# Modulation vectors: four column-tiled rows and a transpose in place of sixteen one-column matmuls

## What is computed

```python
def modulation(cond, w_ada, b_ada):
    m = jax.nn.silu(cond) @ w_ada + b_ada
    return [t[..., None, :] for t in jnp.split(m, 6, axis=-1)]

def modulate(h, shift, scale):
    return h * (1 + scale) + shift
```

## Time and profile before

| | us |
|---|---|
| median of 3 runs | 2021.09 |
| lowest, highest | 2018.03, 2022.53 |
| the profiled execution, its device time | 2019.94 |
| its span, first to last instruction | 2018.1 |
| PE busy | 1816.4 (90%) |
| DVE busy | 1369.9 (68%) |
| ACT busy | 799.4 (40%) |
| POOL busy | 153.7 (8%) |

### The profile page before, as it was taken

How to read it: one execution, slowest core, us unless ns; L and a number is a source line. 1 busy time by engine, 2 the same in 40 slices (tenths; PEclk the granted TensorE clock), 3 DMA queues, 4 the chain that set the end, 5 groups by cost and what they waited for, 6 DMA issues and landing times. The chain is left out here.

```text
span 2018.1 us, 28781 instructions
## 1 busy us (share of the span) xinstructions
PE 1816.4 (90%) x11914; PEld 1623.7 (80%) x11914; DVE 1369.9 (68%) x1856; ACT 799.4 (40%) x1138; POOL 153.7 (8%) x156
## 2 busy tenths in 40 slices
PE   5788989899999999779899998955899999898999
PEld 1578668678788878676789998954899999788999
DVE  2596565889966775664567666889787876755544
ACT  1321454343213431334455455352443434445452
POOL 0123100011000110141001010001000001100000
PEclk9778679899999999787999999986899999889999
DMA  6342100334364445330034644623687885313552
GB/s 246 142 167 87 60 1 22 146 145 162 141 233 186 181 162 194 128 142 25 10 131 149 205 145 161 251 102 122 236 328 296 327 323 186 109 53 136 189 185 86
DMA packets 46658, 317.87 MB, mean 158 GB/s; under 512 B 5248, under 2 KB 6272, under 8 KB 12608
## 3 DMA queue, kind: packets, MB, share of 16 engines
q1 hardware_dynamic: 45936, 312.22, 42.2%
q0 software_dynamic: 592, 3.81, 0.5%
HBM read 314.96 MB, written 1.05 MB: 157 GB/s over the span
## 5 line engine op out<-in xcount | busy, mean ns | idle before, releaser
L1375 PE MATMUL PM<-Hhi,whi 128*128 128x256 f32 (+1 forms) x1766 | 567.3, 321 | 72.3 <-DVE Hlo L1247 31.0
L1376 PE MATMUL PM<-Hlo,whi 128*128 128x256 f32 (+1 forms) x1766 | 554.8, 314 | 0.0
L1377 PE MATMUL PM<-Hhi,wlo 128*128 128x256 f32 (+1 forms) x1766 | 554.8, 314 | 0.0
L873 DVE TENSOR_TENSOR wlo<-raw,whi 128x2048 fp32r<-128x2048 f32 (+3 forms) x205 | 443.0, 2161 | 139.2 <-ACT whi L621 138.9
L621 ACT ACTIVATE whi<-raw 128x2048 fp32r<-128x2048 f32 (+3 forms) x205 | 365.2, 1781 | 187.0 <-PE PM L1377 159.1
L1375 PEld LDWEIGHTS PM<-Hhi,whi 128*128 128x128 f32 x1766 | 344.8, 195 | 102.0 <-issue 53.6
L1376 PEld LDWEIGHTS PM<-Hlo,whi 128*128 128x128 f32 x1766 | 346.4, 196 | 17.0 <-issue 0.2
L1377 PEld LDWEIGHTS PM<-Hhi,wlo 128*128 128x128 f32 x1766 | 345.6, 196 | 17.6
L902 DVE SCALAR_TENSOR_TENSOR acc<-raw,silc,acc 128x512 f32<-128x512 f32 x384 | 286.1, 807 | 1.6 <-DVE wlo L873 0.2
L1375 PE MATMUL PM<-Ghi,whi 128*128 128x256 f32 (+1 forms) x864 | 270.8, 313 | 11.7 <-DVE Glo L1099 11.7
L1376 PE MATMUL PM<-Glo,whi 128*128 128x256 f32 (+1 forms) x864 | 265.7, 308 | 0.0
(11 more groups left out here) (186 smaller groups left out, 1998.2 us busy)
## 6 DMA issues: line engine op xcount, KB each, us to landing
raw<-in_ada SPq DMA_DIRECT2D x104, 1024.0 KB, 4.8
raw<-in_wm SPq DMA_DIRECT2D x91, 1024.0 KB, 4.9
raw<-in_wl SPq DMA_DIRECT2D x68, 1024.0 KB, 4.9
raw<-in_wl SPq DMA_DIRECT2D x32, 704.0 KB, 4.4
raw<-in_wm SPq DMA_DIRECT2D x8, 704.0 KB, 4.1
raw<-in_wm SPq DMA_DIRECT2D x4, 768.0 KB, 4.9
X<-in_x SPq DMA_DIRECT2D x1, 2048.0 KB, 9.4
bias<-in_bias POOLq DMA_DIRECT2D x1, 2048.0 KB, 11.2
```

Source lines behind the costliest of these rows:

```text
L873: dve.tensor_tensor(wslot(wlo, i, usize(u)), slot_raw(n, usize(u)), wslot(whi, i, usize(u)).bitcast(F32), ALU.subtract)\
L1375: pe.matmul(out, st_hi, mv_hi, start=first, stop=False)
L1376: pe.matmul(out, st_hi, mv_lo, start=False, stop=False)
L1377: return pe.matmul(out, st_lo, mv_hi, start=False, stop=last)
```

## The change

The two halves of a vector are now summed together. The four slots of `acc` are summed over the partitions as four rows: for each slot one matmul with a 128 x 32 block of ones as weights and the slot's 512 columns as moving operand, written to its own 32 partitions of one PSUM bank (`ada_rows`, one call for a vector). ACT copies the bank to a new buffer `rsum`. One unit later PE transposes the four 128 x 128 blocks of `rsum` (`ada_columns`), so that the sums stand on the partitions, and DVE adds the bias; for vectors with two partial sums it now adds the two on the columns. Pieces 16 to 19 move: two behind unit 8 and two behind unit 9, where there were one, one, and two behind unit 10. The first piece of a vector now waits for the rows of the one before, since all four slots are read at once; before, it waited for the `ada_sum` two halves back. The diff below is in the order of the file: the plan, then ACT (behind `evac(u)`), DVE (`ada`, then `ada_done`) and PE.

```diff
+    n[8] = n[9] = 2
+    n[10] = 0
...
-REDUCE_AT = [[a // 2 for a in (ADA_AT[i - 1] if i else []) if a % 2] for i in range(NU)]
+ROWS_AT = [[a // 4 for a in (ADA_AT[i - 1] if i else []) if a % 4 == 3] for i in range(NU)]
+COLUMNS_AT = [ROWS_AT[i - 1] if i else [] for i in range(NU)]
...
+                    for v in ROWS_AT[i]:
+                        act.wait_ge(*at("aux", ("rows", v)))
+                        if v > 2:
+                            act.wait_ge(*at("aux", ("ada", v - 1)))
+                        act.activation(rsum[:, :], aux(("rows", v)), ACT.Copy).then_inc(*tick("aux_act", ("rows", v)))
...
-                if part == 0 and hv >= 2:
-                    dve.wait_ge(*at("aux", ("ada", hv - 2)))
+                if part == 0:
+                    dve.wait_ge(*(at("aux", ("rows", v - 1)) if v > 2 else at("aux", ("ada", ("first", 3)))))
...
+                each = view(aux(key), "p (k h w z) -> p h w k z", k=4, h=2, w=2)[:, :, :, :, 0]
+                srcv, odd = each[:, :, 0:nw], each[:, :, 1:2]
+                for h in range(2):
+                    ins = dve.tensor_tensor(dst[:, h], srcv[:, h], bia[:, h].unsqueeze(1).to_broadcast([P, nw, 4]), ALU.add)
+                if nw == 1:
+                    ins.then_inc(*C.link("dve_chain"))
+                    dve.wait_ge(*C.last)
+                    for h in range(2):
+                        ins = dve.tensor_tensor(dst[:, h], dst[:, h], odd[:, h], ALU.add)
...
-            def ada_sum(hv):
+            def ada_rows(v):
+                key = ("rows", v)
+                dst = take(key)
+                for hv in (2 * v, 2 * v + 1):
+                    pe.wait_ge(*at("raw_used", RAW_AT["ada", 2 * hv + 1]))
+                for r in range(4):
+                    ins = pe.matmul(dst[32 * r:32 * r + 32, :], ones[:, 0:32], acc[:, r * 512:r * 512 + 512], start=True, stop=True)
+                ins.then_inc(*tick("aux", key))
+
+            def ada_columns(v):
+                key = ("ada", v)
+                dst = take(key)
+                pe.wait_ge(*at("aux_act", ("rows", v)))
                 for c in range(4):
-                    for who in range(2):
-                        a = (hv % 2) * 1024 + who * 512 + c * 128
-                        if v < CTXV:
-                            ins = pe.matmul(dst[:, who * 4 + c:who * 4 + c + 1], acc[:, a:a + 128], ones[:, 0:1], start=True, stop=True)
-                        else:
-                            ins = pe.matmul(dst[:, c:c + 1], acc[:, a:a + 128], ones[:, 0:1], start=(who == 0), stop=(who == 1))
+                    ins = pe.transpose(dst[:, c * 128:c * 128 + 128], rsum[:, c * 128:c * 128 + 128], ident)
                 ins.then_inc(*tick("aux", key))
...
-                    for hv in REDUCE_AT[i]:
-                        ada_sum(hv)
+                    for v in ROWS_AT[i]:
+                        ada_rows(v)
+                    for v in COLUMNS_AT[i]:
+                        ada_columns(v)
```

More of the change, by code:

```diff
@@ L224, in ada_plan @@
     for st in ("L0", "L1", "M1"):
-        assert sum(n[:first_of("out", st)]) % 2 == 0
+        at_attn = first_of("out", st)
+        assert (len(ADA_FIRST) + sum(n[:at_attn])) % 4 == 0 and n[at_attn - 1] == n[at_attn - 2] == 0
     return out
@@ L907, in ada, with mod_of, ada_first_done @@
                         marks[half] = C.last
-            def ada_done(hv):
+            def mod_of(v):
+                base = {0: 0, 1: 6, 2: 12, 3: 18, 4: 20}[0 if v < 6 else 1 if v < 12 else 2 if v < 18 else 3 if v < 20 else 4]
+                return MODTYPE[v - base]
+            def ada_first_done(hv):
                 v, half = hv // 2, hv % 2
-                key = ("ada", hv)
+                key = ("ada", ("first", hv))
+                dve.wait_ge(*at("aux", key))
+                dst = view(mod[:, v * 16:v * 16 + 16], "p (w k) -> p w k", w=2)[:, :, half * 4:half * 4 + 4]
+                srcv = view(aux(key, 0, 8), "p (k w) -> p w k", w=2)
+                bia = feat[:, FEAT["bada"] + v * 8 + half * 4:FEAT["bada"] + v * 8 + half * 4 + 4].unsqueeze(1).to_broadcast([P, 2, 4])
+                dve.tensor_tensor(dst, srcv, bia, ALU.add).then_inc(*tick("aux_dve", key))
+                if mod_of(v) == "scale":
+                    dve.wait_ge(*at("aux_dve", key))
+                    g = feat[:, FEAT["norm"] + half * 4:FEAT["norm"] + half * 4 + 4].unsqueeze(1).to_broadcast([P, 2, 4])
+                    dve.scalar_tensor_tensor(out=dst, in0=dst, scalar=1.0, in1=g, op0=ALU.add, op1=ALU.mult)\
+                        .then_inc(*tick("mod", v if half else ("half", v)))
@@ L913, in ada_done @@
+            def ada_done(v):
+                key = ("ada", v)
                 dve.wait_ge(*at("aux", key))
                 nw = 2 if v < CTXV else 1
[L915 to L922, removed]
+                dst = view(mod[:, v * 16:v * 16 + 8 * nw], "p (w h k) -> p h w k", w=nw, h=2)
+                each = view(aux(key), "p (k h w z) -> p h w k z", k=4, h=2, w=2)[:, :, :, :, 0]
@@ L923, in ada_done @@
+                ins.then_inc(*tick("aux_dve", key))
+                if mod_of(v) == "scale":
                     norm = {1: 0, 4: 1, 7: 2, 10: 3, 13: 4, 16: 5, 19: 6, 21: 7, 24: 8}[v]
-                    ins.then_inc(*tick("aux_dve", key))
                     dve.wait_ge(*at("aux_dve", key))
-                    g = feat[:, FEAT["norm"] + norm * 8 + half * 4:FEAT["norm"] + norm * 8 + half * 4 + 4].unsqueeze(1).to_broadcast([P, nw, 4])
-                    ins = dve.scalar_tensor_tensor(out=dst, in0=dst, scalar=1.0, in1=g, op0=ALU.add, op1=ALU.mult)
@@ L928, in ada_done @@
-                    ins.then_inc(*tick("mod", v if half else ("half", v)))
-                else:
-                    ins.then_inc(*tick("aux_dve", key))
+                    g = feat[:, FEAT["norm"] + norm * 8:FEAT["norm"] + norm * 8 + 8].unsqueeze(1).to_broadcast([P, nw, 8])
+                    both = view(mod[:, v * 16:v * 16 + 8 * nw], "p (w k) -> p w k", w=nw)
+                    dve.scalar_tensor_tensor(out=both, in0=both, scalar=1.0, in1=g, op0=ALU.add, op1=ALU.mult).then_inc(*tick("mod", v))
```

13 lines of the change are left out of this document (6 added, 7 removed).

## The result

| | before | after |
|---|---|---|
| median of 4 runs, us | 2021.81 | 1966.17 |
| lowest, highest | 2018.03, 2023.91 | 1965.05, 1967.2 |
| profiled execution, its device time | 2019.94 | 1967.2 |
| its span | 2018.1 | 1965.4 |
| mean granted clock over the span | 0.915 | 0.924 |

The ratio of after to before is 0.9727, with a 95% interval of 0.971 to 0.9744: about 55 us faster. The direction was right; the forecast of 1980 and the low end of its range, 1971, were both too high. Between the profiled executions the gain is 52.7 us, where the sum gave 39.8.

The account below looks back on a forecast made before the run. PE, busy 90% of the span, was taken as the bound in most stretches. Saving 34.3 us there plus 7 in L0's projections, less 0.5 and 1, gave 39.8: from 2019.94 to 1980 us, own range 1971 to 1990, with rivals to 2009.

Parts of the forecast that it names:

- the 34 old calls that were priced: One-column reduction calls in PE-bound stretches, taken at 1.78 us each; with one more at 0.8, 60.5 us.
- the five in L0's `up`: Old reduction calls in a DVE-bound stretch, 420 to 536 us, where a shorter PE gains nothing: worth 0.
- Rival 1: Column tiles overlap only in part: 19 to 29 us more than forecast, 1999 to 2009 us; chance 0.15.
- rival 2: fp32 column tiles don't overlap at all, rows cost 3.65 us, slower than before: 2037 us; chance 0.13.
- Rival 3: In M0's MLP and KV, DVE or the DMAs become the bound, 16 us lost: 1996 us; chance 0.08.
- Step (a): L0's projections, call at 131.57: rows of vector 2 take 2.0 us instead of 3.22; 1.3 us gained.
- Step (b): L0's projections, behind unit 4: no reduction there any more, so unit 5 starts at 166.2, 4.8 us earlier.
- R: PE time of one vector's rows, four column tiles together: 1.07 us at full clock, bounds 0.9 and 3.65.
- The break-even: Price of a vector's rows at which the time equals the old kernel's: near 2.9 us.
- unit 156: The call behind it, ahead of a norm, covers DVE and ACT work awaited anyway: 0.8 us, not 1.78.
- (c): L0's projections, call at 200.50: rows of vector 3 take 2.0 us instead of 3.41; 1.4 us gained.
- the 1 us set aside: Allowance for added ACT copies, DVE sums and waits, and DMA share, otherwise counted as covered: 1 us.

Follow-up runs that it names:

- e3: Changed kernel with the four row matmuls writing the same 128 partitions one after the other, 128 columns of ones as weights: 2022.06 us, ratio 1.0002 to the kernel before.
- e1: The changed kernel again, unchanged, for a second profile: 1965.94 us, ratio 0.973 to the kernel before.
- e5: Kernel before with the one reduction behind unit 4 moved behind unit 5: 2012.85 us, ratio 0.9969.
- e6: Kernel before with only pieces 16 to 19 placed as in the change: 2020.6 us, ratio 1.0009.
- e2: Changed kernel with the eight row matmul records issued twice: 1986.16 us, ratio 0.983 to the kernel before.
- e9: Kernel before with one more DVE memset over 1024 columns ahead of the first projection unit, about 0.9 us: 2018.22 us, ratio 0.9979.
- e10: Kernel before with one more DVE memset over 2048 columns ahead of the first projection unit, about 1.8 us: 2020.6 us, ratio 0.9991.
- e8: The kernel before again, unchanged, for a second profile: 2018.87 us, ratio 0.9997.
- e11: Changed kernel with one more DVE memset over 1024 columns ahead of the first projection unit: 1966.92 us, ratio 0.9727 to the kernel before.
- e12: Changed kernel with one more DVE memset over 2048 columns ahead of the first projection unit: 1966.4 us, ratio 0.9723 to the kernel before.
- e14: Changed kernel with the four transposes of one vector moved from behind unit 41 to behind unit 42: 1973.58 us, ratio 0.9771 to the kernel before.
- e7: Kernel before with each reduction cut from 8 one-column matmuls to 1, vectors wrong: 1951.84 us, ratio 0.9677.
- e13: Kernel before with one call of ada_sum moved from behind unit 42 to behind unit 43: 2016.9 us, ratio 0.9982.
- e4: Changed kernel with only the first of the four row matmuls, 128 columns of ones, other slots left out: 1962.85 us, ratio 0.9712 to the kernel before.

## Why the prediction was off

**Right.** The bound and the counts: the 34 old calls that were priced are on the path, none of the five in L0's `up` is. The tiles: the records start in two groups of four, 0.46 us apart, the next unit's load 1.00 us behind the first (forecast 1.07). The transposes 0.43. Rival 1 and rival 2 fell; e3 is rival 2 made real, and it ends at the time of before, not above it. Rival 3 did not occur in M0's MLP. Step (a): PE got to unit 3 1.3 us earlier, as forecast (0.7 in e1). Step (b), 4.8 us at unit 5: measured 4.8, and e5 shows it alone. The moved pieces: at most 0.3 in e6, 0.5 forecast.

**The price of rows, mis-sized against the change.** I took R from load to load. On the path the rows cost 1.19 and not 1.07, because turning costs 0.34 and not 0.2; 18 times 0.12 is 2.2 us of gain less. Eight old calls in M0 cost 1.87 and not 1.78, 0.7 us the other way.

**The break-even, mis-sized.** I gave 2.9 us for R. e3, at 3.43, ends level. By the slope of 24 measured in e2, (3.43 - 1.19) x 24 is 54 us, all of the gain. The break-even was low because the rest of the gain was larger than I had it. (The low end of the forecast's own range does not follow from its terms either: 1980.1 - 3 - 5 is 1972, not 1971.)

**Rival 3's mechanism, at a place I had not named.** In the recurrent stage I counted 4.1 us gained and 1.5 came. Up to `lgate` and in `lout` 4.7 us was gained, and 1.5 went back to the wait for `wlo` and 1.6 ahead of the norm. The earlier trace rows count calls by stretch and do not show what waits behind them: I should have followed each stretch to the next wait, as I did for unit 156.

**A call put at nothing.** The forecast gave 0 to the call "in L1 behind a wait for POOL". PE behind unit 55, in before and in after:

```profile
896.29 0.93 PE L1452 MATMUL PX<-cst,zu 128*128 128x128 f32 x4 [3.20 <-POOL zu L564]
897.02 3.47 PE L1467 MATMUL PX<-cst,acc 128*128 128x1 f32 x16
900.34 0.56 PE L1375 MATMUL PM<-whi,Hhi 128*128 128x256 f32 x1
```

```profile
868.23 1.11 PE L1484 MATMUL PX<-cst,zu 128*128 128x128 f32 x4 [3.21 <-POOL zu L570]
869.27 1.94 PE L1495 MATMUL PX<-acc,cst 128*32 128x512 f32 x8
871.14 0.47 PE L1407 MATMUL PM<-whi,Hhi 128*128 128x256 f32 x1
```

The wait stands ahead of the transposes; the call comes behind it, at half clock, and unit 56 starts when it ends. It took 3.32 us, the rows take 1.87: 1.4 us gained on the path.

**The step that failed: the clock was held fixed.** The sum gave ordinary work the time that it took at the clock it had before; (a) and (c) priced their rows at half clock. Most of the surplus sits where that clock changed:
- L0's projections, 2.8: the rows of vector 3 took 1.00 at full clock where I had 2.0 at half, and units 5 and 7 took 12.4 and 11.4 us where they had taken 13.5 and 12.6.
- units 42 and 43: 3.3.
- L1: 3.7. Unit 56 is 1.1 of it; attention 1.6, chance (e1); the call put at nothing 1.4, less 0.4 for the transposes that stand there now.
- unit 125: 1.3, which e9 and e10 also get without the change; unit 159: 1.5 (clock 0.79 before, 1.00 after), which e10 gets without it.
- M1: 1.9, chance (e8).

These make 14.5 us. With unit 24 (0.5, half clock again), the 1 us set aside and 0.9 at units 8 to 13, and less the 2.6 given back and the net price error of 1.5, it is 12.8; the surplus was 12.9. The medians differ by 3 us more than the profiled executions do; no trace tells where that lies.

Is this the change's merit? In part. The clock's share in the projections, at unit 24, in units 42 and 43 and at unit 56 (2.8 + 0.5 + 3.3 + 1.1 = 7.7 us) recurs in e1, e11 and e12, so it is not chance; 2.8 us (units 125 and 159) the kernel before gets by a shift of 1 or 2 us, and 3.5 (attention and M1) is chance. And it is a matter of the plan more than of the tiles: e14 has the same reductions and is 7 us slower, e5 has the old ones and one of them moved, and its attention in L1 takes 2.5 us more, and e7, with light old calls, has half clock at unit 43. What stays open is which detail decides at unit 42: PE waits 3.01 or 3.02 us where the clock fell fully or in part (before, e5, e7, e13, e14) and 2.95 where it did not (after, e2, e3), but e4 waited 2.95 and lost some 3 us of full clock. The place of the calls on either side of the wait moves this too (e13), and no run separates the two.

The range was too narrow for the same reason. It had 5 us for the cold stretch of the projections and nothing for the rest of the 343 us at half clock.

**The tiles against the two rules of the prediction.** The Trainium skill, TensorE: Matmul & The Clock Gate, Measured speedup vs the span model, gives 2.38 times for three column tiles. Here four fp32 tiles of 512 columns took 0.85 us (e2) where four matmuls in one place take 3.43 (e3): 4 times, and 2.9 times (3.43/1.19) with the turning counted, so the 1.1 us estimated by it did not come. The Trainium skill, the same page, The mechanism, has weight loads overlap with running matmuls only where the row group differs; here all eight loads, of 0.106 to 0.109 us each, in the same rows and four quarters of the columns, are over within 0.16 us, so R was not the 2.35 of that rule.

## What to carry to other kernels

A sum over the partitions of several 512-column pieces is cheap as ones matmuls in different column quarters: four for the price of one, plus about a third of a microsecond for turning to tiles and back, to be read from the matmuls on both sides and not from load to load. Where a share of the run is at half clock, a change of PE's plan moves it, and one moved set of four transposes was worth 7 us of 1966; give the range that much on both sides. Before counting a PE gain as won, follow PE to its next wait; and before counting it as nothing, see whether the call stands ahead of the wait or behind it.

## What the runs showed of the hardware

- Four 128 x 32 tiles with all 128 partitions streaming did not slow each other down: 0.85 us for two steps of four records of 512 fp32 columns (e2); one 128-wide matmul costs 0.86 to 0.94 (e4).
- At half clock (131.41 and 869.27 in after) the eight records took 1.90 and 1.87 us to the next load, against 1.00 at full clock.
- A call of 16 one-column records, 8 matmuls, costs 1.78 to 1.87 us, one of 2 records 0.23 to 0.31: about 0.11 us for each record of one column. The four records of 128 columns of a set of transposes cost as much each (0.43 for four).
- PE's clock fell around a wait of 3 us in one plan and stayed up in another: 3.01 us and 2.95 us in e14 and in after, whose work differs by the place of four transposes.
- Work that was not changed took longer far behind a change: L1's attention 90.3 us in e5 and 87.8 in before, with one call moved 750 us earlier (one profile).
